# The gate projection of the latent branch moves from the end of one unit into the score tiles of its own

## The chip, the cores and the metric

The kernel runs on one NeuronCore of a Trainium2 chip. The metric is the device time of one execution in microseconds. Before the change it was 4350.89 us (median of three runs, 4349.49 to 4351.80).

## The reference

The input x (512 tokens of 1024 features) first passes a block with two attentions (dilated and two-dimensional neighbourhood) and a feed-forward part, and then two hybrid layers that also read a context of 256 tokens. Each layer projects the normalised tokens and runs three attention branches of width 1024; each branch is gated, projected, and merged. The change is almost all in the first branch, called mla (latent attention, 8 heads):

```
q  = (rms_norm(qc, q_norm) @ w_uq)    # per head 64 features plus 32 that are rotated
kv = (rms_norm(kvc, kv_norm) @ w_ukv) # per head 64 key features and 128 value features
s  = (q * 96**-0.5) . k               # keys: 512 latent tokens and 256 context tokens
o  = softmax(s) @ v                   # per head [tokens, 128]
y  = o * silu(z)                      # z = normalised tokens @ 128 columns of w_in per head
```

In the first layer the queries are all 768 tokens (six tiles of 128 queries, here called items), in the second only the 512 latent ones (four items). All is float32. A projection with the large matrices is done with three matmuls for each product (high times high, low times high, high times low), for which ScalarE (ACT) makes the high part of a weight tile and VectorE (DVE) the low part.

## The kernel before, in words

The program is a list of stages (`plan`, L119), each with its part on TensorE (PE), ACT, DVE and the DMA queue SP (SyncE). Every stage ends in a fence of the engines (L2292). The order of the work on each engine is the order in which the Python code issues it, and semaphores tie the engines together; nothing is scheduled by a planner, except that `done_by` (L727) says how many steps of a side task PE issues after each group of scores.

A stage "units" runs heads one after another: a prologue (projections of unit 0), a loop of steps (unit i, with the projections of unit i+1 beside it) and an epilogue (the last unit, nothing beside it). For mla there are eight units: a prologue, seven steps, an epilogue, in each of the two layers. The parts of a step on PE (`pe_units`, L1462 on), for unit i:

1. `pe_scores` (L731): for each item a score tile of 512 and 256 key columns, three matmuls each, into the PSUM banks 4 and 5 or 6 and 7 in turn. From the third group on, PE waits until ACT has taken the tile of two groups back (`exped`, L743). After each group it issues some side steps, and after the last group all that are left. The side steps are `qk_steps` of unit i+1 (L1018): the query projection (three K tiles, into banks 0 and 1) and the key projection (two K tiles, into banks 2 and 3). In front of the keys PE waits for `z_ev`, the gate of unit i having left banks 2 and 3 (L1026).
2. `pe_values` (L879): it waits until all probabilities are normalised, turns them chunk by chunk through PSUM (4 transposes, ACT or DVE copies them back in turn) and multiplies each with V. After the second turn it issues `pe_rope` (L1060), one matmul that rotates the queries of unit i+1 and waits for `rope_in`. Beside the products from the fourth on it issues one step of `v_steps` (the V projection of unit i+1, L1085) each. Steps that are left follow.
3. `pe_proj_z` (L1114): the gate projection of unit i+1 into banks 2 and 3: 8 K tiles, three matmuls each, of 512 columns and, in the first layer, again of 256.

ACT in a step (`act_units`, L1551): the exponentials of the items (L778); then `act_proj_qk` (L1132), which waits for the keys (`kv_ev`) and copies first the queries to SBUF (L1139) and then the keys' high part (L1141), after which `rope_in` is given; the copies of turned chunks 0, 2, 4, 6 (L993) with the queries' high part after chunk 4 (L1175); then `act_proj_z` (L1267): the high part of the next gate weight (L545) and the tanh of the gate (L1280), which waits for the gate's matmuls.

DVE in a step (`dve_units`, L1639): for each item the maximum (L803), and one item later the normalisation (L818, L821); the copies of chunks 1, 3, 5, 7 (L995), after chunk 1 the keys' low part (L1222) and the rotation (L1209 to L1212), after chunk 5 the queries' low part (L1196); the output (L1335); the copy of V (L1262); then `dve_proj_z` (L1283): the low part of the next gate weight (L555), and the gate's last step (L1293), which waits for the tanh.

In the stages dil and na of the first block, which have the same frame, the prologue's `act_proj_v` (L1236) makes the high part of weight 3, which is the first weight of unit 1, before it copies V's projection (L1244), and `dve_proj_v` (L1249) the low part before it copies the turned V (L1262). PE turns V in between (L1111) and then starts the scores.

## Time and profile before

| | |
|---|---|
| profiled execution, its own time | 4348.03 us |
| its span, first to last instruction | 4346.2 us |
| PE busy (matmul) | 3848.7 us, 89% |
| DVE busy | 2169.5 us, 50% |
| ACT busy | 1385.1 us, 32% |
| mean granted clock of TensorE | 0.948 |

How it is read: times are in microseconds from the start of the span. A row of the timeline has the start, the duration, the engine, the line, the operation, its output and inputs, how many alike follow each other, and in brackets how long the engine sat idle before it and what ended that. The granted clock is 1.00 at 2.4 GHz and 0.50 at 1.2 GHz. Matmuls are pipelined, so the distance of two starts tells more than a duration.

### The profile page before, as it was taken

What the parts mean: (1) busy time and instruction counts of PE and PEld (TensorE: products, weight loads), DVE (VectorE), ACT (ScalarE), POOL (GpSimd) and SP (SyncE); (2) the same over time, 40 slices, a digit from 0 to 9 for tenths busy, and PEclk for the clock granted to TensorE, in tenths of its full rate; (3) what the DMA queues carried; (4) which work ended last, traced back from release to release, by engine and by line L of the source; (5) the groups of instructions that cost most, each with busy time, mean ns of one, the idle gap of its engine ahead of it and who ended that gap; (6) DMA issues with size and microseconds to landing.
All of it is one profiled execution on the core that took longest, in us unless ns stands there. A gap on an engine that the chain in (4) does not pass through costs nothing. (4 is left out here: it accounts for less than half of the span.)

```text
span 4346.2 us, 56051 instructions
## 1 busy us (share of the span) xinstructions
PE 3848.7 (89%) x20877; PEld 2933.9 (68%) x20877; DVE 2169.5 (50%) x3457; ACT 1385.1 (32%) x2472; POOL 0.2 (0%) x4
## 2 busy tenths in 40 slices
PE   5988979997689999999798998976999999798898
PEld 2655758875466687777586766864667777576666
DVE  2555346543445525777524554243553677535544
ACT  2433233322223313444312433121332444314432
POOL 0000000000000000000000000000000000000000
PEclk8998989998799999999899999987999999899999
DMA  6443335531101021111121101211013121121122
GB/s 232 137 117 93 87 88 161 170 110 62 35 25 29 15 68 40 38 39 39 30 63 34 29 26 30 68 39 38 26 30 87 44 52 39 49 68 35 35 59 73
DMA packets 504242, 275.36 MB, mean 63 GB/s; under 512 B 56665, under 2 KB 489781, under 8 KB 504094
## 3 DMA queue, kind: packets, MB, share of 16 engines
q1 hardware_dynamic: 483186, 252.08, 20.7%
q10 hardware_dynamic: 20908, 21.26, 1.6%
q8 instruction: 99, 1.62, 0.2%
q14 instruction: 49, 0.40, 0.0%
HBM read 271.08 MB, written 10.32 MB: 65 GB/s over the span
## 5 line engine op out<-in xcount | busy, mean ns | idle before, releaser
L559 PE MATMUL ps<-h_high,w_high 128*128 128x512 f32 (+1 forms) x3512 | 1313.0, 374 | 165.8 <-DVEq L2294 129.8
L559 PE MATMUL ps<-h_low,w_high 128*128 128x512 f32 (+1 forms) x3512 | 1280.4, 365 | 0.0
L559 PE MATMUL ps<-h_high,w_low 128*128 128x512 f32 (+1 forms) x3512 | 1278.0, 364 | 0.0
L559 PEld LDWEIGHTS ps<-h_high,w_high 128*128 128x128 f32 x3512 | 673.4, 192 | 318.0 <-DVEq L2294 137.2
L555 DVE TENSOR_TENSOR w_low<-w_raw,w_high 128x1024 fp32r<-128x1024 f32 x378 | 453.6, 1200 | 629.9 <-ACT w_high L545 605.8
L559 PEld LDWEIGHTS ps<-h_high,w_low 128*128 128x128 f32 x3512 | 672.2, 191 | 106.6
L559 PEld LDWEIGHTS ps<-h_low,w_high 128*128 128x128 f32 x3512 | 673.8, 192 | 98.6 <-issue 2.2
L545 ACT ACTIVATE w_high<-w_raw 128x1024 fp32r<-128x1024 f32 x378 | 392.3, 1039 | 789.5 <-PE ps L559 606.2
L778 ACT ACTIVATE probs<-ps,neg_max 128x768 f32<-128x768 f32 (+2 forms) x368 | 289.1, 788 | 492.9 <-DVE neg_max L803 291.0
L559 PE MATMUL ps<-k_high,q_high 64*128 64x256 f32 (+4 forms) x784 | 189.9, 402 | 136.9 <-ACT probs L778 78.7
L559 PE MATMUL ps<-probsT,v 128*128 128x512 f32 (+4 forms) x736 | 287.5, 560 | 8.8 <-DVE probsT L995 8.6
L803 DVE TENSOR_REDUCE neg_max<-ps 128x1 f32<-128x768 f32 (+1 forms) x240 | 195.0, 846 | 113.5 <-PE ps L559 100.3
L559 PEld LDWEIGHTS ps<-k_high,q_high 64*128 64x128 f32 (+1 forms) x784 | 92.1, 193 | 228.8 <-ACT probs L778 118.1
L559 PE MATMUL ps<-y_high,w_high 128*128 128x512 f32 (+1 forms) x640 | 229.7, 359 | 1.3 <-ACT y_high L1971 1.1
L559 PE MATMUL ps<-y_low,w_high 128*128 128x512 f32 (+1 forms) x640 | 228.9, 358 | 0.0
L559 PE MATMUL ps<-y_high,w_low 128*128 128x512 f32 (+1 forms) x640 | 228.6, 357 | 0.0
L559 PE MATMUL ps<-y_and_merged 128*128 128x128 f32 (+4 forms) x656 | 168.0, 390 | 21.3 <-DVEq L2294 17.0
L799 DVE TENSOR_REDUCE row_max<-ps 128x1 f32<-128x512 f32 (+2 forms) x160 | 110.0, 688 | 149.3 <-PE ps L559 149.1
L887 PEld LDWEIGHTS ps<-ident,probs 128*128 128x128 f32 x832 | 103.2, 145 | 94.6 <-issue 77.5
L559 PE MATMUL ps<-k_low,q_high 64*128 64x256 f32 (+4 forms) x784 | 157.6, 333 | 0.0
L559 PE MATMUL ps<-k_high,q_low 64*128 64x256 f32 (+4 forms) x784 | 157.1, 332 | 0.0
L1978 ACT ACTIVATE probs<-ps 128x512 f32<-128x512 f32 x88 | 44.8, 538 | 336.3 <-PE ps L559 336.2
(200 smaller groups left out, 4034.7 us busy)
## 6 DMA issues: line engine op xcount, KB each, us to landing
w_raw<-in_w_in SPq DMA_DIRECT2D x444, 256.0 KB, 3.2
y_and_merged<-in_w_mod SPq DMA_DIRECT2D x96, 256.0 KB, 3.2
w_raw<-in_w_branch SPq DMA_DIRECT2D x96, 256.0 KB, 3.1
w_raw<-in_w_up SPq DMA_DIRECT2D x88, 256.0 KB, 4.2
y_and_merged<-in_w_ada SPq DMA_DIRECT2D x64, 256.0 KB, 3.3
w_raw<-in_w_out SPq DMA_DIRECT2D x48, 256.0 KB, 3.1
w_raw<-in_w_down SPq DMA_DIRECT2D x44, 256.0 KB, 3.0
y_and_merged<-in_w_ada SPq DMA_DIRECT2D x4, 2048.0 KB, 20.3
```

Source lines behind the costliest of these rows:

```text
L545: act.activation(WR[:, k, 0:nk], WRAW[:, k, 0:nk], ACT.Copy).then_inc(s_high, 1)
L555: nc.vector.tensor_tensor(WL[:, k, 0:nk], WRAW[:, k, 0:nk], WR[:, k, 0:nk].bitcast(F32), ALU.subtract).then_inc(s_low, 1)
L559: return nc.tensor.matmul(*a, **kw)
L778: act.activation(it["dst"], src, ACT.Exp, bias=NM[:, idx:idx + 1], accum_out=SL[:, idx:idx + 1]).then_inc(S["exped"], 1)
L799: v.tensor_reduce(MX[:, idx:idx + 1], src, AXX, ALU.max, negate=True)
L803: v.tensor_reduce(NM[:, idx:idx + 1], src, AXX, ALU.max, negate=True).then_inc(S["maxed"], 1)
L887: last = nc.tensor.transpose(PS[:, b:b + 128], tile, ident[:, :])
L1978: last = act.activation(d, p, ACT.Tanh, scale=0.5)
```

## The change

In mla the gate projection of a unit no longer stands at the end of the step before. Its steps (`mla_z`) are now the first side steps among the unit's own score groups, ahead of the query and key projection of the next unit; in the epilogue they are the only side steps, and in the prologue the gate is gone. PE waits for `kv_low` (new: the low part of the keys is made, so that banks 2 and 3 are free) before the first. ACT issues its part of the gate (`act_proj_z`) after the exponential of item `z_group`, DVE its part (`dve_proj_z`) after the maximum of that item and the normalisation of the item before; `z_group` comes out as item 3 of 0 to 5 in the first layer and as item 2 of 0 to 3 in the second. In the epilogue both do it after all items. `done_by` for mla has all but the last four side steps issued by the last group but one.

The query copy on ACT waits for `q_mm` (the query matmuls) instead of the keys, and gives `q_out` at once; the rotation matmul on PE waits for `q_out` instead of `rope_in`. The V projection of the next unit stands behind the values' last product on PE, not beside the products.

In the prologues of dil and na, ACT's high part and DVE's low part of weight 3 now follow the V copies.

```
@@ done_by
-            return max(n_side - TAIL, 0) * (group + 1) // (s["items"] // (2 if paired(s) else 1))
+            groups = s["items"] // (2 if paired(s) else 1)
+            if s["name"] == "mla":
+                return min(max(n_side - TAIL, 0) * (group + 1) // (groups - 1), max(n_side - TAIL, 0))
+            return max(n_side - TAIL, 0) * (group + 1) // groups
@@ dve_softmax, one item after another
                 if idx and s["name"] not in SCALED_LAST:
                     normalise(idx - 1)
+                after(idx)
@@ z_group
-            return min(g for g in range(s["items"] // 2) if done_by(s, nz + side_plan(s)[0], g) >= nz)
+            return min(g for g in range(s["items"] // (2 if paired(s) else 1)) if done_by(s, nz + side_plan(s)[0], g) >= nz)
@@ pe_rope
-            pe.wait_ge(S["rope_in"], cnt(s, "rope_in", t, ui, u + 1))
+            key = "q_out" if name == "mla" else "rope_in"
+            pe.wait_ge(S[key], cnt(s, key, t, ui, u + 1))
@@ act_proj_qk
+                act.wait_ge(S["q_mm"], cnt(s, "q_mm", t, ui, u + 1))
+                for d, p in evac_cols(s, 0, Q, cq, slice(0, 96)):
+                    last = act.activation(d, p, ACT.Copy, scale=sc)
+                last.then_inc(S["q_out"], 1)
                 act.wait_ge(S["kv_ev"], cnt(s, "kv_ev", t, ui, u + 1))
-                for d, p in evac_cols(s, 0, Q, cq, slice(0, 96)):
-                    act.activation(d, p, ACT.Copy, scale=sc)
@@ act_proj_v
-            if first:
+            if first and not s["first"]:
                 act_high(act, s, t, s["nh"], 3)
...
-            if s["first"] and not first:
+            if s["first"]:
                 act_high(act, s, t, s["nh"], 3)
@@ dve_proj_v
-                if s["first"] or first:
+                if s["first"] != first:
                     dve_low(dve, s, t, s["nh"], 3)
...
+            if s["first"] and first:
+                dve_low(dve, s, t, s["nh"], 3)
@@ pe_units
-                pe_proj_z(pe, s, 0, 0, 0)
+                if name == "diff":
+                    pe_proj_z(pe, s, 0, 0, 0)
...
+            def mla_z(t, u, i):
+                pe.wait_ge(S["kv_low"], cnt(s, "kv_low", t, 2, u + 1))
+                yield from split_steps(pe, s, t, 2, u, 128, tgroups(2, s["cq"]))
+            def mla_side(t, u, i):
+                yield from mla_z(t, u, i)
+                yield from qk_steps(pe, nxt, t, u, i + 1, True)
...
+                if name == "mla":
+                    pe_scores(pe, s, t, u, i, 0, mla_side(t, u, i), nz + n_side)
+                    pe_values(pe, s, t, u, i, 0, lambda: pe_rope(pe, nxt, t, u, name))
+                    for _ in v_steps(pe, nxt, t, u, i + 1):
+                        pass
+                    return
... (epilogue)
+                elif name == "mla":
+                    pe_scores(pe, s, t, u, i, 0, mla_z(t, u, i), nz)
@@ act_units and dve_units, in the step
+            def mla_z(t, u, i, idx):
+                if idx == z_group(s):
+                    act_proj_z(act, s, t, u, i)      # dve_proj_z on DVE
```

## Rows read from the trace of the kernel before

**Rows 1.** Windows: busy time of each engine, granted clock (PEclk), DMA share, GB/s.

```profile
1265.00:1301.00 36.00, 34.06 (x175) 24.14 (x174) 18.65 (x34) 11.22 (x25) 0.00 (x0) 1.00 0.09 25
...
700.00:800.00 100.00, 100.00 (x666) 81.43 (x665) 58.66 (x71) 34.90 (x48) 0.00 (x0) 1.00 0.57 164
```

**Rows 2.** Waits of PE, first layer's steps (two rows), second layer's (two rows).

```profile
PE ps L559 <- ACT probs L778: 9.7, 14, 0.9
PE ps L559 <- ACT k_high L1141: 4.7, 7, 0.7
...
PE ps L559 <- ACT probs L778: 4.7, 6, 1.0
PE ps L559 <- ACT k_high L1141: 2.4, 6, 0.4
```

**Rows 3.** Timeline of PE, first layer: a gate, then the next unit.

```profile
1292.28 0.48 PE L559 MATMUL ps<-h_high,w_high 128*128 128x512 f32 x1
...
1297.84 0.28 PE L559 MATMUL ps<-h_high,w_high 128*128 128x256 f32 x1
...
1300.71 0.40 PE L559 MATMUL ps<-k_high,q_high 96*128 96x512 f32 x1
...
1311.29 3.32 PE L559 MATMUL ps<-y_and_merged 128*96 128x256 f32 x10
...
1314.55 1.09 PE L887 MATMUL ps<-ident,probs 128*128 128x128 f32 x8
...
1316.32 1.10 PE L559 MATMUL ps<-qT,rot_mla 96*96 96x512 f32 x2 [0.68 <-ACT k_high L1141]
...
1327.24 1.05 PE L559 MATMUL ps<-y_and_merged 128*128 128x128 f32 x8
```

**Rows 4.** Timeline of ACT and DVE in the same unit.

```profile
1300.99 0.87 ACT L1280 ACTIVATE y_and_merged<-ps 128x512 f32<-128x512 f32 x2 [10.82 <-PE ps L559]
...
1301.89 1.02 DVE L1293 SCALAR_TENSOR_TENSOR y_and_merged<-y_and_merged,ps 128x512 f32<-128x512 f32 x2 [6.81 <-ACT y_and_merged L1280]
...
1303.49 1.82 DVE L803 TENSOR_REDUCE neg_max<-ps 128x1 f32<-128x768 f32 x2 [0.57 <-issue]
...
1309.79 0.90 ACT L778 ACTIVATE probs<-ps,neg_max 128x768 f32<-128x768 f32 x1 [0.92 <-DVE neg_max L803]
...
1312.88 0.35 DVE L821 TENSOR_SCALAR probs<-probs,exp_sum_inv 128x256 f32<-128x256 f32 x1
```

**Rows 5.** Page, costliest groups: busy, mean ns, idle before, releaser.

```profile
L555 DVE TENSOR_TENSOR w_low<-w_raw,w_high 128x1024 fp32r<-128x1024 f32 x378 | 453.6, 1200 | 629.9 <-ACT w_high L545 605.8
...
L545 ACT ACTIVATE w_high<-w_raw 128x1024 fp32r<-128x1024 f32 x378 | 392.3, 1039 | 789.5 <-PE ps L559 606.2
```

**Rows 6.** Timeline of PE, first layer: a score group after a wait.

```profile
1305.52 0.50 PE L559 MATMUL ps<-k_high,q_high 96*128 96x512 f32 x1 [0.82 <-ACT probs L778]
...
1305.86 0.40 PE L559 MATMUL ps<-k_low,q_high 96*128 96x512 f32 x1
```

**Rows 7.** Timeline of PE, first layer's epilogue: first score matmul, first turn.

```profile
1478.41 0.40 PE L559 MATMUL ps<-k_high,q_high 96*128 96x512 f32 x1
...
1490.71 1.97 PE L887 MATMUL ps<-ident,probs 128*128 128x128 f32 x8 [1.74 <-DVE probs L821]
```

**Rows 8.** Window inside that epilogue.

```profile
1486.00:1488.00 2.00, 1.05 (x4) 0.76 (x4) 1.92 (x5) 0.99 (x2) 0.00 (x0) 0.50 0.00 0
```

**Rows 9.** Timeline of PE, second layer's epilogue: first score matmul, first turn.

```profile
3238.67 0.40 PE L559 MATMUL ps<-k_high,q_high 96*128 96x512 f32 x1
...
3248.23 1.70 PE L887 MATMUL ps<-ident,probs 128*128 128x128 f32 x8 [3.55 <-DVE probs L821]
```

**Rows 10.** Timeline, prologue of dil (two rows) and of na (one row).

```profile
105.20 1.06 ACT L545 ACTIVATE w_high<-w_raw 128x1024 fp32r<-128x1024 f32 x1 [11.79 <-DMA w_raw<-in_w_in]
...
109.42 0.79 PE L559 MATMUL ps<-h_high,w_high 128*128 128x512 f32 x1
...
266.00 0.69 DVE L1262 COPY v<-ps 128x512 f32<-128x512 f32 x1 [6.06 <-PE ps L1111]
```

More of the change, by code:

```diff
@@ L151, in add @@
             now[k] = now.get(k, 0) + v
-    keys = ("h n square square_mm rstd scaled high x_t mm_ev rope_in rope_mm roped q_mm k_mm q_out kv_ev vt_in vt_mm v_ev z_ev tanh scores maxed exped normed "
+    keys = ("h n square square_mm rstd scaled high x_t mm_ev rope_in rope_mm roped q_mm k_mm q_out kv_ev kv_low vt_in vt_mm v_ev z_ev tanh scores maxed exped normed "
             "pt_act pt_dve rl_mm transposed o_done o_sq o_ss o_rs y bias merged up_ev gelu f_high f_low y_low y_high m_high m_low out_ev ctx_in mod_copy mod_sum qk_high qk_low").split()
@@ L176, in plan @@
             if s["name"] == "mla":
-                add(s, q_mm=n, k_mm=n, kv_ev=n, v_ev=n, z_ev=n, tanh=n, rope_mm=n, roped=n)
+                add(s, q_mm=n, q_out=n, kv_ev=n, kv_low=n, v_ev=n, z_ev=n, tanh=n, rope_mm=n, roped=n)
             if s["name"] == "diff":
@@ L1021, in qk_steps @@
                     for kc in range(3):
-                        mm(ps, WN[:, k, 96 * kc:96 * kc + 96], M[:, kc, lo:lo + n], start=kc == 0, stop=kc == 2)
+                        last = mm(ps, WN[:, k, 96 * kc:96 * kc + 96], M[:, kc, lo:lo + n], start=kc == 0, stop=kc == 2)
+                        if kc == 2 and (lo > 0 or not cq):
+                            last.then_inc(S["q_mm"], 1)
                         yield
@@ L1221, in dve_proj_qk @@
                     h = KH[0:64, 0:LAT] if d.shape[1] == LAT else KH[0:64, LAT:TOK]
-                    nc.vector.tensor_tensor(d, p, h.bitcast(F32), ALU.subtract)
+                    last = nc.vector.tensor_tensor(d, p, h.bitcast(F32), ALU.subtract)
+                last.then_inc(S["kv_low"], 1)
                 dve_rope(dve, s, u, t, ui, Q[0:96, 0:LAT], 96, 0, TAB["cos_mla"][:, :], TAB["sin_mla"][:, :])
@@ L1374, in moved @@
             m.base = dict(s.base)
-            for key, per in (("h", s["nh"]), ("n", s["nn"]), ("v_ev", 1), ("vt_in", 1), ("vt_mm", 1), ("z_ev", 1), ("q_out", 1), ("rope_in", 1), ("tanh", 1), ("kv_ev", 1),
+            for key, per in (("h", s["nh"]), ("n", s["nn"]), ("v_ev", 1), ("vt_in", 1), ("vt_mm", 1), ("z_ev", 1), ("q_out", 1), ("q_mm", 1), ("rope_in", 1), ("tanh", 1), ("kv_ev", 1), ("kv_low", 1),
                              ("qk_high", 1), ("qk_low", 1), ("roped", 2 if s["name"] == "diff" else 1), ("rope_mm", 2 if s["name"] == "diff" else 1), ("y", s["subs"])):
@@ L1540, in prologue @@
                 act_proj_v(act, s, 0, 0, 0, True)
-                if name != "swa":
+                if name not in ("mla", "swa"):
                     act_proj_z(act, s, 0, 0, 0)
@@ L1554, in mid @@
                         swa_z(t, u, i, idx)
+                    if name == "mla":
+                        mla_z(t, u, i, idx)
                     if name == "diff" and idx == side_plan(s)[1] - 1:
@@ L1584, in step @@
                         act_mod(act, s, i, s["nn"], e, 1, 384)
-                act_proj_z(act, nxt, t, u, i + 1)
+                if name != "mla":
+                    act_proj_z(act, nxt, t, u, i + 1)
             def epilogue(t, u, i):
                 act_exps(act, s, t, u, i, 0, splits(s, nxt, t, u, 0) if name == "swa" else [])
+                if name == "mla":
+                    act_proj_z(act, s, t, u, i)
                 if name == "swa":
@@ L1625, in dve_units, with mla_z @@
             nxt = moved(s)
+            def mla_z(t, u, i, idx):
+                if idx == z_group(s):
+                    dve_proj_z(dve, s, t, u, i)
             def swa_z(t, u, i, idx):
@@ L1635, in prologue @@
                 dve_proj_v(dve, s, 0, 0, 0, True)
-                if name != "swa":
+                if name not in ("mla", "swa"):
                     dve_proj_z(dve, s, 0, 0, 0)
@@ L1651, in step @@
                 dve_bias(dve, s, i)
-                dve_softmax(dve, s, t, u, i, 0, splits(s, nxt, t, u, 0), (lambda idx: swa_z(t, u, i, idx)) if name == "swa" else lambda idx: None)
+                dve_softmax(dve, s, t, u, i, 0, splits(s, nxt, t, u, 0), (lambda idx: (swa_z if name == "swa" else mla_z)(t, u, i, idx)) if name in ("mla", "swa") else lambda idx: None)
                 if name == "swa":
@@ L1665, in step @@
                     dve_proj_v(dve, nxt, t, u, i + 1)
-                dve_proj_z(dve, nxt, t, u, i + 1)
+                if name != "mla":
+                    dve_proj_z(dve, nxt, t, u, i + 1)
             def epilogue(t, u, i):
@@ L1670, in epilogue @@
                 dve_softmax(dve, s, t, u, i, 0, splits(s, nxt, t, u, 0) if name == "swa" else [])
+                if name == "mla":
+                    dve_proj_z(dve, s, t, u, i)
                 if name == "swa":
```

## The prediction

> **What bounds the kernel now.** I read the windows by stage first. In a step of the first mla stage PE is busy 34.06 of 36 us at a granted clock of 1.00, while DVE has 18.65 and ACT 11.22 [rows 1]: PE is the bound, and only its idle time can be won. The list of who waited for whom, taken over seven steps of each layer, says what that idle time is [rows 2]. In the first layer it is 9.7 us in 14 waits of score groups for an exponential (0.69 each, two a unit) and 4.7 us in 7 waits of the rotation matmul for ACT's key copy (0.67 each). In the second it is 4.7 us in 6 (0.78 each, one a unit) and 2.4 us in 6 (0.40 each). So a unit idles 2.06 us in the first layer and 1.18 us in the second; nothing else of note. The reader is to see that seven steps of each layer hold at most 14.4 and 8.3 us. The timeline then shows the edges: in the epilogues no side steps stand between the score groups, and PE idles with its clock down (their rows stand with the edges below).
>
> **The prices on PE.** A gate takes from 1292.28 to 1300.71, 8.43 us: 24 matmuls of 512 columns until 1297.84 (5.56 us, 0.23 each, 0.70 a step of three) and 24 of 256 (2.87 us, 0.12 each, 0.36 a step) [rows 3]. A score tile has the same columns (three of 512, three of 256): 1.05 us, or 0.36 for the 256-column tiles of the context's queries. The plain projections cost more: after the last group, one query step of 256 and four key steps (two of 512, two of 256) take from 1311.29 to 1314.55, 3.26 us for 1792 columns, so 0.93 for 512 and 0.47 for 256 [rows 3]. The keys are 2.8 us, the queries 4.2 in the first layer and 2.8 in the second.
>
> **The prices beside PE.** Maximum 0.91 (1.82 for two), exponential 0.90 and some 0.1 to its sum, tanh 0.87, last gate step 1.02, last normalisation of 256 columns 0.35 [rows 4]; high part 1.04, low part 1.20 [rows 5]. For the 512 columns of the second layer I take 0.60 for the tanh and 0.69 for the last step (estimates, two thirds).
>
> **A step of the first layer, laid out anew.** I write it from the first score matmul (0). Side steps by the new rule: 4, 4, 5, 4, 5 of 26 after the groups, then 4. Tile 0 to 1.05, four gate steps to 3.8; tile 1 and four to 7.7; tile 2 to 8.7 and five short ones to 10.5; tile 3 to 11.6, three gate steps (gate done at 12.7) and a query step to 13.6; tile 4 and five query steps to 17.2; tile 5 to 17.5; the keys to 20.3. Exponential 0 is over at 3.1, 2 at 10.7, 3 at 13.6: every group finds its bank free, so the two waits of 0.69 go. On ACT, after exponential 3: high part to 14.7, tanh to 15.5. On DVE: low part to 15.9, last step to 17.0. The keys may thus start at 17.0, and PE gets there at 17.5: no wait, 0.5 us to spare. Queued behind the gate's block on DVE are the maxima of items 4 and 5 and the last three normalisations: 17.4, 18.1, 18.5, 19.0, 19.8. PE asks for the probabilities at 20.3. Before, they were ready at 1313.2 against 1314.55 [rows 3, 4]; the slack shrinks from 1.3 to 0.5 us.
>
> The rotation: ACT is through with exponential 5 at 19.2, the query copy (0.86, as the tanh of the same columns) ends at 20.1, and PE's first two turns end at 21.2. The 0.67 us goes. The key copy moves behind it, 20.4 to 21.2, then chunk 0's copy to 21.8; PE's rotation ends at 22.1, so nothing new is late there, by 0.3 us.
>
> The V projection beside the products did no waiting of its own; its place at the end costs what it covered: chunk 7's short copy after a short product. I take 0.3 us for that and 0.1 for latencies elsewhere. At the end its 12 matmuls (four of them 1.05 us at most, 2.6 in all [rows 3]) cover the output on DVE (1.02), for which the next unit's scores wait; the copy of V ends as tile 0 does. PE also restarts slowly after a wait: its second matmul starts 0.34 after the first instead of 0.23 [rows 3, 6], so two restarts less are 0.2 more. So: 2.06 - 0.4 + 0.2, 1.9 us a step. Bounds: 0.9 (the two slacks of 0.5 missed by 0.5 each) and 2.3. Times seven: 13.3 us, from 6 to 16.
>
> **A step of the second layer.** Four tiles, 15 side steps: 3, 4, 4, 0, then 4. Tile 2 ends at 8.1, the last gate step at 8.8, three query steps at 11.6, tile 3 at 12.6. Exponential 2 ends at 10.2, high part 11.2, low part 12.5, last step 13.2: here the keys wait, 0.6 us. Maximum 3, exponential 3, its normalisation: 14.1, 15.1, 16.1, while the keys end at 16.0: another 0.1 to 0.2. So 0.8 us of new waiting against 1.18 and a restart of 0.1: 0.5 us a step, 3.4 us in all. Bounds: minus 0.5 a step (the block 1 us longer) and 1.2 (none of it felt): -3 to 8.
>
> This wait is DVE's order: the maximum of tile 3 stands behind the gate's last step. That is seen before too: tile 0 is complete 1.05 after 1300.71, but its maximum starts at 1303.49, behind the gate's step of 1301.89 [rows 3, 4].
>
> **The edges.** The prologues lose the gate: 8.4 and 5.6 us; the weight of unit 1 loses its early split and gains a later one, under scores. In the epilogues it fills waits. First layer before: 12.30 us from first score to first turn, with the clock at 0.50, so that eight transposes take 1.97 instead of 1.09 and the first product about 0.9 more [rows 3, 7, 8]: 14.1 in full-clock terms. After: side steps 2, 2, 3, 2, 3, then 4; PE is through at 13.5, the probabilities at 13.7. But ACT's gate part comes after all exponentials: high part until 14.1, tanh 15.0, chunk 0's copy 15.6, where PE wants it at 14.6; 0.2 more for chunk 1 behind DVE's low part and last step. That is 15.0, or +0.9: net -7.5 us. Second layer: 9.56 plus about 1.6 for the low clock [rows 9] against 10.0 plus 0.5: -0.7, net -6.3. Together 13.8 us; bounds 10 and 16.
>
> On the clock the trace shows 1.00 through steps that idle 0.7 to 1.0 us at a time [rows 1, 2], and 0.50 in the epilogue with its longer idling [rows 8]. With waits of about 1 us I count the new epilogues at full clock. The Trainium skill, in "TensorE: Matmul & The Clock Gate", section "What's actually happening", says that throttled is the default state and that recent activity releases it. By that rule a thin stretch can lose the clock without one long gap, which speaks against my count; the sum would then be some 3.5 us smaller.
>
> **Dil and na.** In dil's prologue ACT waited 11.79 us for weight 3's DMA, with V's copy queued behind. Now V, its turn and the first scores run during that wait. The next unit's projection then starts when weight 3 is split: 105.20 + 1.06 + 1.2 = 107.5 instead of 109.42 [rows 5, 10]: -1.9 us (0 to -3). In na the weight was there early; its low part of 1.2 us now stands on DVE behind V's copy, in front of the first maxima, and in front of PE's side steps [rows 5, 10]: +1.2 us (0 to 2.5). Together -0.7.
>
> **Sum.** 13.3 + 3.4 + 13.8 + 0.7 = 31.2 us. The profiled execution took 4348.03 (span 4346.2 and 1.8 around it), so 4316.8; the median of the runs shown lies 2.9 higher: 4320 us.
>
> **Rivals.**
> - *All waiting goes.* The gate's block is felt nowhere: 16 + 8 in the steps, 14 at the edges: 38 us, 4313. For it: 0.5 us of slack in the first layer. Against: the second layer's chain is longer than its cover by 0.6.
> - *Only the edges gain.* The waits in the steps are replaced by others as long (keys on `z_ev`, turns on the last normalisation): 14.5 us, 4336. For it: both slacks are near 0.5 us. Against: each link of the chain has a row.
> - *Slower: the gate's block becomes the path.* High part, low part, tanh and last step (1.04 + 1.20 + 0.87 + 1.02 = 4.1 us) run with nothing beside them in each unit, in front of the keys. The point is where the query steps that PE has left after the gate are shorter than the block and the softmax tail. A step would gain 2.06 and lose 4.1 in the first layer, 1.18 and 3.5 in the second: 14 + 16 = 30 us lost, 14.5 gained: 4366. Against: 4.6 us of scores and queries lie between the gate's end and the keys in the first layer, 3.8 in the second.
> - *A denser PE loses its clock.* Against: 100 us of 100 busy ran at 1.00 [rows 1]. At 0.50 for a tenth of the 14 steps (some 45 us at full speed) it would take 45 us more and make the kernel slower; I count it in the 0.03 of slower.
>
> **Chances.** Forecast (4310 to 4328) 0.68; all waiting goes 0.10; only the edges 0.17; slower 0.03; something between, no change, 0.02. A difference of 0.2%, 8.7 us, is about what can be told from no change. Faster 0.94, same 0.03, slower 0.03. The range 4309 to 4337 takes in the first two rivals.
>
> **What would show it.** In the first layer PE's waits for exponentials are nearly gone and a unit is 1.9 us shorter; the wait of the rotation is gone in both; the second layer shows a wait of the keys for L1293 of about 0.6 and a unit shorter by 0.5. The epilogue's clock stays at 1.00, with a wait of a product for L993 or L995 near 1 us. Dil's first scores come near 102. I am wrong if the waits reappear under L1293 or L821 with more than 1 us a unit.

## The result, and the profile after

The kernel after took 4307.39 us (median of four runs, 4305.82 to 4307.58) where the kernel before, on the same chip, took 4351.35 (4349.49 to 4357.63). The ratio is 0.9895, with a 95% interval from 0.988 to 0.991: 44 us faster. The forecast was 4320 with a range from 4309 to 4337, so the direction came out, most of the mechanisms did, and the size was 13 us too small. The profiled execution took 4305.82 us (span 4304.0); against the span of before that is 42.2 us, where the sum had 31.2.

The first view of the kernel after is the page's head: the span, then for each engine its busy time, share and instructions. The matmuls are as many as before. PE's busy time fell by 16.6 us, with the mean granted clock from 0.948 to 0.951; the other 25.6 of the 42.2 us were idle time. ACT is busy for 6.2 us more, 5.1 of them in four more loads of its function table (1.28 us each, two in each mla stage).

```profile
span 4304.0 us, 56060 instructions
...
PE 3832.1 (89%) x20877; PEld 2926.4 (68%) x20877; DVE 2169.0 (50%) x3457; ACT 1391.3 (32%) x2476; POOL 0.2 (0%) x4
```

To find the time I cut both traces at the fences of the stages and, inside the two mla stages, at the first score matmul of each of the eight units. The table gives us; "rest" is the span without the two mla stages. Such starts repeat: in a second profiled execution of the kernel after (e13 below) the two stages came out at 273.18 and 230.17.

| | before | after | change | forecast |
|---|---|---|---|---|
| layer 1: fence to first scores | 27.59 | 16.03 | -11.56 | -8.4 |
| layer 1: a unit, mean of seven | 35.49 | 33.02 | -2.47 | -1.9 |
| layer 1: last unit to the fence | 24.96 | 25.96 | +1.00 | +0.9 |
| layer 1: stage | 301.00 | 273.16 | -27.84 | -20.8 |
| layer 2: fence to first scores | 24.07 | 16.52 | -7.55 | -5.6 |
| layer 2: a unit | 28.11 | 27.68 | -0.43 | -0.5 |
| layer 2: last unit to the fence | 20.46 | 19.90 | -0.56 | -0.7 |
| layer 2: stage | 241.29 | 230.16 | -11.13 | -9.7 |
| rest | 3803.9 | 3800.7 | -3.2 | -0.7 |

The second view is the waits of PE over the seven steps of each layer, in total us, times, longest. In the first layer the list is empty: the 14 waits for exponentials and the 7 for the key copy [rows 2] are gone. In the second layer those are gone too, and two others stand there, the ones forecast: 0.54 a unit for the gate's last step and 0.24 for the last normalisation.

```profile
PE ps L559 <- DVE y_and_merged L1306: 3.8, 7, 0.5
PE ps L891 <- DVE probs L824: 1.7, 7, 0.3
```

The third view is the timeline of one unit of the second layer, all engines, in order of start. The gate's last step on DVE ends at 3015.56 and the keys start at 3015.61; behind that step stand on DVE the maximum of the last item, its normalisation, and behind that the turns. The rotation (3019.59) has no wait.

```profile
3012.66 1.04 ACT L545 ACTIVATE w_high<-w_raw 128x1024 fp32r<-128x1024 f32 x1
...
3013.61 0.59 ACT L1293 ACTIVATE y_and_merged<-ps 128x512 f32<-128x512 f32 x1
3013.74 1.23 DVE L555 TENSOR_TENSOR w_low<-w_raw,w_high 128x1024 fp32r<-128x1024 f32 x1 [1.24 <-ACT w_high L545]
...
3014.88 0.68 DVE L1306 SCALAR_TENSOR_TENSOR y_and_merged<-y_and_merged,ps 128x512 f32<-128x512 f32 x1
...
3015.61 2.79 PE L559 MATMUL ps<-y_and_merged 128*64 128x512 f32 x8 [0.54 <-DVE y_and_merged L1306]
3015.73 0.96 DVE L806 TENSOR_REDUCE neg_max<-ps 128x1 f32<-128x768 f32 x1 [0.17 <-issue]
...
3018.66 1.09 PE L891 MATMUL ps<-ident,probs 128*128 128x128 f32 x8 [0.25 <-DVE probs L824]
...
3019.59 1.02 PE L559 MATMUL ps<-qT,rot_mla 96*96 96x512 f32 x2
```

The epilogues keep their clock. These windows (columns as in [rows 1]) of the first layer's epilogue have 1.00 where the window of before had 0.50 [rows 8], and the turns at 1462.36 take 1.09 for eight instead of 1.97 [rows 7]. The products behind them wait for the copies of ACT and DVE, with 0.47 and 0.16 us listed. By the starts it is 0.7 and 0.4: the first product stands 1.57 us behind the first turn, where eight turns at 0.11 would make 0.88, and the second turned pair 1.72 behind the first, where one further on has 1.30. The forecast had charged 1.0 and 0.2 for the two.

```profile
1458.00:1460.00 2.00, 2.00 (x18) 1.91 (x17) 1.91 (x5) 1.09 (x3) 0.00 (x0) 1.00 0.03 8
...
1462.00:1464.00 2.00, 1.22 (x10) 0.93 (x9) 1.65 (x3) 1.88 (x4) 0.00 (x0) 1.00 0.00 0
```

```profile
1462.36 1.09 PE L891 MATMUL ps<-ident,probs 128*128 128x128 f32 x8 [0.31 <-DVE probs L824]
1463.93 1.12 PE L559 MATMUL ps<-probsT,v 128*128 128x512 f32 x2 [0.47 <-ACT probsT L997]
1465.65 1.13 PE L559 MATMUL ps<-probsT,v 128*128 128x512 f32 x2 [0.16 <-DVE probsT L999]
```

The last view is the prologue of the first layer. The rotation starts straight behind the keys, and V's 24 records take 2.94 us at a clock of 1.00.

```profile
1207.04 3.53 PE L559 MATMUL ps<-y_and_merged 128*96 128x256 f32 x11
1210.50 1.10 PE L559 MATMUL ps<-qT,rot_mla 96*96 96x512 f32 x2
1214.60 2.94 PE L559 MATMUL ps<-y_and_merged 128*128 128x128 f32 x24 [3.00 <-DVE qT L1222]
```

The questions were four: what made the first layer's prologue 3.2 us better than the gate's 8.4; what made a unit of the first layer 0.6 better than forecast; what the two small parts (V, dil and na) are worth; and whether the waits left in the second layer can go.

### The profile page after: what moved, and what is told of

Same layout as the page of the kernel before. It is cut to its first block and busy times, and to the rows that moved or that the text cites. A ratio compares the mean times of both kernels' runs of the same rounds, so it can differ in the third digit from the quotient of the medians.

```text
span 4304.0 us, 56060 instructions
## 1 busy us (share of the span) xinstructions
PE 3832.1 (89%) x20877; PEld 2926.4 (68%) x20877; DVE 2169.0 (50%) x3457; ACT 1391.3 (32%) x2476; POOL 0.2 (0%) x4
## 5 line engine op out<-in xcount | busy, mean ns | idle before, releaser
L559 PE MATMUL ps<-y_and_merged 128*128 128x128 f32 (+4 forms) x656 | 152.4, 384 | 26.8 <-DVEq L2341 17.0
```

Of the source, the lines that this page charges most:

```text
L559: return nc.tensor.matmul(*a, **kw)
```

## The experiments

The first four ran on one chip and share the runs of the kernel before (median 4350.33), so do the next four (4355.59) and the last three (4352.64). This table has what the texts below refer to, in us, cut as above; "ratio" is to the kernel before on the same chip, and L1 and L2 are here the first and the second layer.

| | time | ratio, 95% interval | L1 fence to scores | L1 unit | L1 stage | L2 fence to scores | L2 unit | L2 stage | rest |
|---|---|---|---|---|---|---|---|---|---|
| e1 dil and na only | 4351.37 | 1.0000 (0.9991 to 1.0009) | | | 300.97 | | | 241.38 | 3808.0 |
| e2 after, queries late | 4325.75 | 0.9945 (0.9931 to 0.9959) | 19.18 | 33.98 | 282.97 | 18.08 | 28.07 | 234.45 | 3806.6 |
| e3 after, V beside | 4312.87 | 0.9917 (0.9904 to 0.9931) | 16.01 | 33.32 | 275.22 | 16.51 | 27.49 | 228.83 | 3804.7 |
| e4 after, tanh first | 4312.06 | 0.9919 (0.9906 to 0.9933) | 16.07 | 33.02 | 273.54 | 16.51 | 27.58 | 230.20 | 3806.1 |
| e5 gate only | 4325.19 | 0.9929 (0.9916 to 0.9943) | 19.18 | 34.27 | 285.02 | 18.06 | 27.87 | 233.00 | 3807.5 |
| e6 queries only | 4342.33 | 0.9968 (0.9957 to 0.9979) | 24.49 | 34.60 | 293.07 | 22.10 | 27.57 | 236.85 | 3803.6 |
| e7 prologues wait | 4312.82 | 0.9902 (0.9887 to 0.9917) | 19.22 | 33.03 | 276.39 | 18.06 | 27.75 | 232.16 | 3805.1 |
| e10 gate early | 4302.98 | 0.9882 (0.9867 to 0.9897) | 16.01 | 33.02 | 273.11 | 16.54 | 27.05 | 225.73 | 3803.3 |
| e11 and V beside in L2 | 4306.11 | 0.9890 (0.9874 to 0.9906) | 16.03 | 33.02 | 273.17 | 16.53 | 26.85 | 224.34 | 3805.5 |
| e12 and epilogues | 4319.21 | 0.9919 (0.9905 to 0.9933) | 16.02 | 33.03 | 279.12 | 16.55 | 26.85 | 231.07 | 3808.4 |
| e13 after again | 4308.85 | 0.9901 (0.9885 to 0.9917) | 16.06 | 33.02 | 273.18 | 16.50 | 27.69 | 230.17 | 3799.9 |

### e2: the queries' part taken out

```
-            key = "q_out" if name == "mla" else "rope_in"
+            key = "rope_in"
...
                 act.wait_ge(S["q_mm"], ...)
+                act.wait_ge(S["kv_ev"], ...)
                 for d, p in evac_cols(...):
                     last = act.activation(d, p, ACT.Copy, scale=sc)
                 last.then_inc(S["q_out"], 1)
-
-                act.wait_ge(S["kv_ev"], ...)
```

> The kernel after, but the queries are again copied after the keys, and the rotation waits for the key copy. Theory (a wait costs its listed idle time and some 0.2 us of drain that the list leaves out, and in the first prologue it also keeps the clock down): a unit of the first layer 33.02 -> 33.9 us, one of the second 27.68 -> 28.3, the prologues +3.5 and +1.7 us: 7 x 0.89 + 7 x 0.6 + 5.2 = 15.6 us more than after, 4323. Rival (the prediction as it stood: only the listed idle of the steps, 4.7 + 2.4, nothing in the prologues): 7 us more, 4314.5, prologues within 0.3 of after's 16.03 and 16.52.

The two stages are 14.1 us longer than after (9.8 and 4.3), the time 18 us (its rest is longer too). The theory holds and the rival falls: the prologues lose 3.15 and 1.56 us, the units 0.96 and 0.39. The waits of PE show 5.2 us in seven, 0.74 each, for those 0.96, so 0.22 us of each wait is not in the list.

```profile
PE ps L559 <- ACT k_high L1150: 5.2, 7, 0.7
```

In the second layer the list has almost nothing (0.2 us in one wait) for the 0.39 a unit. Its timeline says why. The idle of a PE row is counted from the modelled end of the matmul before, here 3037.17 + 1.10, and the rotation starts at 3038.41, with no bracket of its own; only the weight load shows the wait. Yet from the turns to the first product it is 2.18 us (3037.17 to 3039.35), and 1.79 in the kernel after, by its own rows 3018.66 and 3020.45. The distance of two starts has the loss, the idle column doesn't.

```profile
3037.17 1.10 PE L891 MATMUL ps<-ident,probs 128*128 128x128 f32 x8 [0.25 <-DVE probs L824]
...
3038.41 0.24 PEld L559 LDWEIGHTS ps<-qT,rot_mla 96*96 96x96 f32 x2 [0.38 <-ACT k_high L1150]
3038.41 1.10 PE L559 MATMUL ps<-qT,rot_mla 96*96 96x512 f32 x2
...
3039.35 1.02 PE L559 MATMUL ps<-probsT,v 128*128 128x512 f32 x2
```

### e7: only the prologues wait for the key copy

```
+        def pe_rope(pe, s, t, u, name, first=False):
...
-            key = "q_out" if name == "mla" else "rope_in"
+            key = "q_out" if name == "mla" and not first else "rope_in"
...
+                if first:
+                    act.wait_ge(S["kv_ev"], ...)
```

> The kernel after, but in the prologues alone the queries are copied after the keys and the rotation waits for the key copy, as before. Theory (this wait brings TensorE's granted clock down in front of V's 24 matmuls, so it costs more than its own length): first layer's prologue 16.0 -> 19.0 us with a window at 0.50 behind the rotation, second layer's 16.5 -> 18.2; units as after; 4312. Rival (the wait costs its length only and the clock stays at 1.00): 16.0 -> 17.9, 16.5 -> 18.2, 4311 with V's records at 2.9 us. The window of the clock tells them apart, not the sum.

The prologues come out 3.19 and 1.54 us longer, and the units as after. In the first layer the wait is back with 1.78 us, and V's 24 records take 4.91 us.

```profile
1213.30 3.54 PE L559 MATMUL ps<-y_and_merged 128*96 128x256 f32 x11
1218.62 1.30 PE L559 MATMUL ps<-qT,rot_mla 96*96 96x512 f32 x2 [1.78 <-ACT k_high L1153]
1222.06 4.91 PE L559 MATMUL ps<-y_and_merged 128*128 128x128 f32 x24 [2.15 <-DVE qT L1224]
```

The windows of e7 show the clock at 1.2 GHz under those records; PE had been busy 1.30 of 2 us and then not at all. In the kernel after it idles 3.00 us in front of V, more than the 2.15 here, and the clock stays at 2.4 GHz. What differs is the idle of 1.78 us ahead of the rotation, with which it is 3.93 us of idle in two pieces instead of 3.00 in one.

```profile
1218.00:1220.00 2.00, 1.30 (x2) 0.24 (x2) 1.06 (x3) 0.56 (x2) 0.00 (x0) 0.85 0.00 0
1220.00:1222.00 2.00, 0.00 (x0) 0.00 (x0) 1.93 (x3) 0.00 (x0) 0.00 (x0) 0.50 0.00 0
1222.00:1224.00 2.00, 1.94 (x9) 1.95 (x10) 0.96 (x2) 1.95 (x2) 0.00 (x0) 0.50 0.00 0
```

```profile
1213.00:1215.00 2.00, 0.40 (x3) 0.40 (x4) 1.47 (x3) 0.42 (x1) 0.00 (x0) 1.00 0.00 0
...
1215.00:1217.00 2.00, 2.00 (x20) 2.00 (x20) 0.96 (x1) 1.70 (x2) 0.00 (x0) 1.00 0.00 0
```

(The second pair is the kernel after.) So the 3.2 us are one wait in the prologue, part of it as lost clock: V's records are 1.97 us longer. They don't simply add to the wait, for the 0.85 us less of waiting in front of V gives some back. All five kernels with the wait have this low clock in the first layer's prologue, and none of the eight profiles without it.

In the second layer it is not so clean. There the clock is at 0.50 under V's first records even in the kernel after, with the same 3.00 us of idle in one piece and none ahead of the rotation; the wait of 1.51 us in e7 makes V's records 5.49 us long instead of 4.57. Why 3.00 us cost the clock in one prologue and not in the other, no run here settles.

```profile
2998.21 4.57 PE L559 MATMUL ps<-y_and_merged 128*128 128x128 f32 x24 [3.00 <-DVE qT L1222]
```

### e6 and e5: the parts alone

e6 is the kernel before with the two edits of the queries (the early copy, the wait on `q_out`).

> The kernel before, with only the queries' part: copied to SBUF as soon as their matmuls are done, the rotation waits for that. Theory (a wait is worth its listed idle and some 0.2 us of drain): the waits of the rotation go in both layers, 0.67 and 0.40 listed, with the drain 0.87 x 7 + 0.6 x 7, and 1.76 + 0.2 and 1.49 + 0.2 in the two prologues: 13.9 us, of which 8 in the first mla stage and 5.9 in the second; 4337. Rival (the listed idle alone): 7.1 + 3.3 = 10.4 us, 4340.5. Second rival (the early copy on ACT delays exponentials or the key copy, so that other waits grow): less than 7 us.

The ratio gives 13.9 us, but the stages only 7.9 and 4.4, 12.4 together where the theory had 8 and 5.9; that the ratio hits the number is chance. The units (-0.89 and -0.54) are as the theory had them. The first prologue is not: it is 3.10 us shorter where the theory had 1.96, since its wait also cost the clock (e7), and the second 1.97 for 1.69. The epilogues are 1.4 and 1.3 us longer than before, though nothing in them is changed; in the first layer's the clock stays low for 5.6 us behind the first turn instead of 3.4. They more than take back what the prologues gained beyond the theory. That the waits for exponentials are still 9.7 us in 14 shows that the early copy does not disturb the exponentials.

e5 is the kernel after less the queries' part, V's move, and dil and na.

```
-                    pe_values(pe, s, t, u, i, 0, lambda: pe_rope(pe, nxt, t, u, name))
-                    for _ in v_steps(pe, nxt, t, u, i + 1):
+                    values = v_steps(pe, nxt, t, u, i + 1)
+                    pe_values(pe, s, t, u, i, 0, lambda: pe_rope(...), values, 3)
+                    for _ in values:
... (and e2's edit; dil and na as before)
```

> The kernel after without three of its parts: the queries are copied after the keys and the rotation waits for the key copy, V of the next unit stands beside the products, dil and na are as before. Only the gate's move is left. Theory (parts add up; queries' part 14 us in the two mla stages, as their removal alone showed, V's part 1 us, dil and na 2 us at most): the mla stages 18 and 8 us shorter than before instead of 27.8 and 11.1, less 2 for V in the first layer, so 24 us faster than before, 4326. Rival (parts cover each other: with the gate gone from the prologue the key copy is what PE waits for, and V beside the products hides part of that wait): the mla stages together at least 5 us off the 24, 4321 or 4331.

The stages are 15.98 and 8.29 us shorter than before, 24.3 together. The theory's sum holds: in the first layer 15.98 for the gate, 9.81 for the queries (e2) and 2.06 for V (e3) make 27.85 of 27.84 measured. In the second 8.29 + 4.29 - 1.33 make 11.25 of 11.13. The gate alone takes 8.41 and 6.01 us from the prologues, against the 8.4 and 5.6 of the forecast, and 1.22 from a unit of the first layer. In that 1.22 a new wait is charged: with V beside the products and no gate behind them, the next unit's scores wait for the output on DVE, 2.9 us in seven.

### e3: V beside the products again

The edit is the first hunk of e5's diff, on the kernel after.

> The kernel after, with the V projection of the next unit beside the values' products again, as before. Theory (from the unit times: the 0.3 us a step that the prediction charged for V at the end did not show): no difference, 4306 to 4308.5, units 33.0 and 27.7 us. Rival A (the charge was real, and something else gained more): 14 x 0.3 = 4 us faster, 4303. Rival B (V at the end is itself a gain, because its evacuation or its 12 matmuls cover the output of DVE before the next scores): a wait of the next unit's scores for DVE's output of up to 0.7 us a unit, 4312 or more.

Neither text fits alone. In the first layer a unit is 0.30 us longer: with V beside the products, the next unit's scores wait for the output on DVE.

```profile
1255.37 0.47 PE L559 MATMUL ps<-k_high,q_high 96*128 96x512 f32 x1 [0.43 <-DVE y_and_merged L1348]
```

In the second a unit is 0.19 shorter, with no such wait: there V at the end is a loss. 2.06 lost and 1.33 won leave 0.7 us; that the time is 5 us above after's is mostly its rest, 3804.7 for 3800.7. The forecast had charged V's move 0.3 a step in the first layer and nothing in the second; e3's text took the charge for both. Rival B is what the first layer shows; its number, 4312 or more, was hit by the rest.

### e1: dil and na alone

The edit is the change's own hunks of `act_proj_v` and `dve_proj_v`, on the kernel before.

> The kernel before, with only the prologues of dil and na changed. Theory (the terms on record): dil 1.9 us shorter, since its first side steps start at 107.5 instead of 109.42, na 1.2 us longer, together -0.7 us, so 4350.6 where the kernel before takes 4351.3. Rival: in the full change dil's stage became 0.5 and na's 1.7 us shorter; if this part did that, the time falls by 2.2 us, and na's first side steps start no later than before.

No difference: 1.0000, from 0.9991 to 1.0009. Dil's stage is 0.4 us shorter (164.54 for 164.93), na's 0.2. Of the waits of PE in dil's stage, the first two here are of the kernel before, the last two of e1.

```profile
PE ps L1111 <- ACT probs L1244: 6.3, 1, 6.3
PE ps L559 <- DVE neg_max L796: 6.1, 3, 2.2
```

```profile
PE ps L559 <- DVE w_low L555: 5.1, 1, 5.1
...
PE ps L1111 <- ACT probs L1244: 0.7, 1, 0.7
```

The wait of 6.3 us became two, 5.1 and 0.7. Dil's first side step starts 1.7 us earlier from the fence (28.6 against 30.3 us), the scores of the later units 1.2 us earlier up to the last unit's (132.3 against 133.6). There the clock takes most of it: it falls to 0.50 at 134.6 us from the fence instead of 138.4, and 0.5 us is left where the last unit's products start.

Na's +1.2 is there too, though its stage hides it. The first side step now stands 2.08 us behind the first scores instead of 0.90, behind a wait for the low part of weight 3 as the prediction has it, and the second and third units start 1.1 and 1.2 us later from the fence than before. The first row is of the kernel before, the others of e1.

```profile
266.79 0.50 PE L559 MATMUL ps<-h_high,w_high 128*128 128x512 f32 x1
```

```profile
263.38 0.50 PE L559 MATMUL ps<-k_high,q_high 64*128 64x512 f32 x2
...
265.46 0.47 PE L559 MATMUL ps<-h_high,w_high 128*128 128x512 f32 x1 [1.11 <-DVE w_low L555]
```

(Before, the first scores start at 265.89.) The last unit starts 0.4 us earlier than before, because in the third unit the kernel before has its clock at 0.50 for a while, 100 us behind the fence, and e1 has not. The two windows are of before and of e1, at the same distance from the fence. All three kernels with na's old prologue (before, e5, e6) have this dip and none of the others.

```profile
344.00:346.00 2.00, 2.00 (x7) 1.51 (x6) 1.69 (x10) 1.63 (x4) 0.00 (x0) 0.50 0.00 0
```

```profile
341.50:343.50 2.00, 2.00 (x11) 1.37 (x9) 1.92 (x6) 0.82 (x3) 0.00 (x0) 1.00 0.00 0
```

So the theory had both mechanisms right, na's with its size and dil's with 1.2 of the 1.9 us. That the two stages together are 0.6 us shorter, for its 0.7, is luck, since the clock moved both. The rival, that na's side steps start no later, falls.

### e4 and e10: the waits left in the second layer

e4 puts, in mla, ACT's tanh ahead of the next weight's high part and DVE's last step ahead of the low part.

```
@@ act_proj_z (the same in dve_proj_z with dve_low)
-            if s["name"] != "swa":
+            if s["name"] == "diff":
                 act_high(act, s, t, per, off + 1)
... (tanh)
+            if s["name"] == "mla":
+                act_high(act, s, t, per, off + 1)
```

> The kernel after, in mla ACT makes the tanh of the gate ahead of the next weight's high part, and DVE the gate's last step ahead of the low part. Theory: the gate leaves banks 2 and 3 about 2.2 us sooner, so the second layer's wait of the keys for the gate's last step (0.55 us listed) and of the turns for the normalisation (0.26) go, with the drain 0.8 to 1.0 us a unit, and each epilogue's chain gets some 1 us shorter: 7 x 0.9 + 2 = 8 us faster than after, 4299. In the first layer a unit stays at 33.0 us, since PE waits nowhere there. Rival: the next weight's split, now behind the gate, is late for the query steps of the side work; PE then waits for w_low instead, as long or longer: 4307 to 4318.

Missed: the time lies in the rival's range, but PE does not wait for the low part of a weight, and of the 4.7 us above the kernel after the rest alone has 5.4. The waits of the keys are gone, but those of the turns have grown from 1.7 to 5.2 us, and a unit is 27.58 instead of 27.68. The epilogues are 0.35 and 0.7 us longer.

```profile
PE ps L891 <- DVE probs L824: 5.2, 7, 0.8
```

The order inside the gate's block doesn't change what stands on DVE ahead of the last maximum. e10 moves the block instead:

```
@@ done_by, for mla
+                up = 0 if s["cq"] else groups - 2
-                return min(max(n_side - TAIL, 0) * (group + 1) // (groups - 1), max(n_side - TAIL, 0))
+                return min((max(n_side - TAIL, 0) * (group + 1) + up) // (groups - 1), max(n_side - TAIL, 0))
```

> The kernel after, with the side steps of mla's second layer rounded up: 4, 4, 3, 0 after the groups instead of 3, 4, 4, 0, so that the gate's steps are done with the second group and ACT and DVE make the gate after item 1 instead of item 2. Theory (the gate's block, high part to last step, stands in front of the last maxima on DVE, and is the cause of both waits left in the second layer): its last step ends near 9.3 us from the first score matmul instead of 13.2, the keys wait no more and the last normalisation is done at 14.9, before the keys end at 15.4. The waits of 0.55 and 0.26 us go, a unit falls from 27.68 to 26.6 us, 7 us in seven, 4300. Rival (DVE's sum of work in front of the turns is the bound, wherever the gate stands, as it was when the tanh went first and the wait went over from the keys to the turns): the wait of the turns grows to 0.7 and the unit stays at 27.6, 4307.

The unit falls to 27.05, by 0.63 us of the 1.08 expected; the stage is 4.4 us shorter than after's. The wait for the gate is gone, that for the last normalisation stays as it was, and the rival falls.

```profile
PE ps L892 <- DVE probs L825: 1.7, 7, 0.2
```

It took 4302.98 us at a ratio of 0.9882 (0.9867 to 0.9897); e7 on the same chip took 4312.82. It has the best time of all kernels here, but its interval overlaps that of the kernel after (0.988 to 0.991, and 0.9885 to 0.9917 in e13).

### e11, e12 and e13

e11 adds V beside the products in the second layer alone.

> The kernel after with the side steps of the second layer rounded up (4, 4, 3, 0, gate made after item 1), and in the second layer alone V of the next unit beside the products. Theory (the two act on different waits): V beside the products saved 0.19 us a unit in the second layer when it was alone and cost 0.30 in the first, where it is left at the end; so the second layer's unit goes from 27.05 to 26.86 us, its stage to 224.4, 1.3 us less. Rival (with the keys on time, the next unit's first scores come earlier and now wait for DVE's output, as in the first layer): unit 27.05 to 27.2.

The unit is 26.85 and the stage 224.34, 1.4 us less than e10, as expected; the time, 4306.11, doesn't show it, since its rest is 2.2 us longer (3805.5 against 3803.3).

e12 moves the gate's block in the epilogues ahead of the last item.

```
-                    pe_scores(pe, s, t, u, i, 0, mla_z(t, u, i), nz)
+                    pe_scores(pe, s, t, u, i, 0, mla_z(t, u, i), nz + TAIL)
@@ the epilogues of ACT and DVE: act_proj_z and dve_proj_z from behind all items to
+                last_z = lambda idx: ... if name == "mla" and idx == s["items"] - 2 else None
```

> As the one before, and in both epilogues of mla all gate steps stand among the score groups and ACT and DVE make the gate after the last item but one, ahead of the last exponential and the last maximum, where they did it after all items. Theory (the epilogue's turns wait for copies queued behind the gate's work): first layer's epilogue 25.96 -> 24.9 us, second's 19.9 -> 19.0, 2 us together. Rival (the last maximum now waits for the gate's last step, and the chain maximum, exponential, normalisation is what the turns wait for): no change or up to 1 us longer each.

Far off: the epilogues are 6.0 and 6.7 us longer (31.92 and 26.56). The rival's mechanism is right and its size isn't. The timeline of the first layer's epilogue shows it. PE is through with its scores at 1469.7. The high part, the low part (1.22) and the last step (1.01) stand ahead of a maximum of 0.42 us for which everything waits, and two normalisations behind that; PE idles 4.40 us, the clock falls and eight turns take 1.97.

```profile
1469.44 0.28 PE L559 MATMUL ps<-k_high,q_low 96*128 96x256 f32 x1
1470.04 0.86 ACT L1294 ACTIVATE y_and_merged<-ps 128x512 f32<-128x512 f32 x2
1470.17 1.22 DVE L555 TENSOR_TENSOR w_low<-w_raw,w_high 128x1024 fp32r<-128x1024 f32 x1 [0.76 <-ACT w_high L545]
1471.32 1.01 DVE L1307 SCALAR_TENSOR_TENSOR y_and_merged<-y_and_merged,ps 128x512 f32<-128x512 f32 x2
...
1472.42 0.42 DVE L807 TENSOR_REDUCE neg_max<-ps 128x1 f32<-128x256 f32 x1
...
1474.12 1.97 PE L892 MATMUL ps<-ident,probs 128*128 128x128 f32 x8 [4.40 <-DVE probs L825]
```

This is the slower rival of the prediction in small: the gate's block on the path with nothing beside it.

e13 is the kernel after, run again.

> The kernel after once more, for two questions. First, how far its stages repeat: theory: the two mla stages at 273.2 and 230.2 within 0.3 us, its units at 33.02 and 27.68. Second, whether the 3.2 us that it gained outside the two mla stages are its own: theory: they are not, stages that the change does not touch come in two lengths 1.5 us apart by the execution, and the rest of the span comes out 3803 to 3808 us instead of 3800.7. Rival: the rest repeats at 3800.7 within 1 us.

The two mla stages repeat within 0.03 us. The rest comes to 3799.9 against 3800.7, inside the rival's 1 us. But that agreement is a sum of differences both ways: four stages of the same code differ by 1.0 to 1.7 us between the two executions (the first block's output stage 46.2 and 47.9, the last part of its feed-forward 127.8 and 126.6, and two behind it). And the whole time of a kernel moves more than that. The four executions of e13 took 4305.1 to 4313.8 us, the eleven of e1 4341.49 to 4354.99; both profiles of the kernel after are of its fastest execution of the four. So whether the 3.2 us outside mla are this kernel's own stays open. What is known of them: 2.3 lie in dil and na, which are 0.5 and 1.7 us shorter in both executions, and na's is the clock's (one low stretch gone and another shorter), against the work's +1.2. The seven other variants of the kernel after that have the change's code in all those stages have 3803.3 to 3808.4. Single stages at the same code mostly differ by 1.3 to 1.7 us between profiles, the output stage by up to 2.8. One is the stage behind the second layer's mla: 93.33 us in the kernel after, 91.72 in e11. These are its windows from 3230, first of the kernel after and then of e11; PE is busy throughout in both, and the clock differs.

```profile
3230.00:3232.00 2.00, 2.00 (x7) 1.53 (x6) 1.83 (x3) 0.00 (x0) 0.00 (x0) 0.59 0.56 133
3232.00:3234.00 2.00, 2.00 (x7) 1.59 (x6) 0.01 (x1) 0.00 (x0) 0.00 (x0) 0.56 0.68 201
```

```profile
3230.00:3232.00 2.00, 2.00 (x11) 1.64 (x10) 1.31 (x2) 0.00 (x0) 0.00 (x0) 1.00 0.87 224
3232.00:3234.00 2.00, 2.00 (x11) 1.65 (x10) 0.00 (x0) 0.00 (x0) 0.00 (x0) 1.00 0.70 210
```

What decides whether the clock falls there isn't settled.

## Why the prediction was too small

Two steps failed: the prologues' term left a wait out, and the steps' term took listed idle time for lost time. The other mechanisms were right. The mis-sized terms went nearly all in one direction, and two came out beyond their own bounds (steps of the first layer 17.3 us, bound 16; the edges 18.7, bound 16). The gap of 11.0 us between the two profiled executions splits into 7.0 in the first layer, 1.4 in the second and 2.5 elsewhere.

- **The prologues: 5.1 of the 11.0 us.** "The prologues lose the gate: 8.4 and 5.6 us" is the first step that failed, by what it left out: it put the queries' wait there at nothing, without a reason. The gate is worth 8.41 and 6.01 (e5). But the queries' edit acts in the prologue as well, where nothing covers the key copy. There it is worth 3.15 and 1.56 us (e2; 3.19 and 1.54 in e7), as much in the first layer as three steps. I had read the waits over the seven steps only. The row of this wait stands in the trace of before: it is 1.76 us, and V's records behind it run at 1.2 GHz.

```profile
1213.44 1.30 PE L559 MATMUL ps<-qT,rot_mla 96*96 96x512 f32 x2 [1.76 <-ACT k_high L1141]
```

- **The steps of the first layer: 4.0 us.** "So a unit idles 2.06 us" and "seven steps hold at most 14.4" took the list of waits for the whole loss: the second step that failed. Cut at starts (means of seven units, before and after), it is 21.99 and 20.04 us from the first score to the first turn, the gate counted in: 1.95 us for two waits listed with 1.38. From the first turn to the first product it is 2.71 and 1.79: 0.92 for one wait listed with 0.67; e2 has 0.96 for 0.74. So removing 2.06 listed was worth 2.87, and 0.2 of the 0.8 more was in the sum, as slow restarts. The trace of before shows it for one wait: from the side step at 1301.76 to the second score matmul it is 1.10 us where nothing waits, and 2.18 from 1303.68 to 1305.86 [rows 6] with 0.82 listed.

```profile
1301.76 1.02 PE L559 MATMUL ps<-y_and_merged 128*96 128x512 f32 x2
...
1302.86 0.40 PE L559 MATMUL ps<-k_low,q_high 96*128 96x512 f32 x1
...
1303.68 1.02 PE L559 MATMUL ps<-y_and_merged 128*96 128x512 f32 x2
```

  The 0.4 charged against it was right: from the first product to the next gate or scores it is 10.80 us before and 11.19 after, 0.39 more. That V at the end saves 0.30 in e3 is no contradiction. Before, the gate stood between the values and the next scores and covered the output on DVE; e3 has neither gate nor V there.
- **The steps of the second layer: the sum right, two of its terms by luck.** Forecast -0.5 a unit, measured -0.43; waits of 0.6 and 0.1 to 0.2 forecast, 0.54 and 0.24 found. The chain high part, tanh, low part, last step, maximum came out link by link, with ends within 0.2 us of the rows of the timeline above, and from the first score to the first turn, the gate counted in, it is 16.17 us before and 16.12 after, for -0.1 forecast. But the rotation's wait was worth 0.65 (2.44 to 1.79) for 0.40 listed, and V at the end costs 0.27 (9.50 to 9.77), which the forecast had at nothing here; the two errors cancel.
- **The epilogues: right**, +1.0 and -0.56 for +0.9 and -0.7. The first turn comes 13.9 us behind the first score for 13.7 forecast, and 10.2 for 10.0. The doubt about the clock did not come true: the trace has 1.00 through both. The Trainium skill's page "TensorE: Matmul & The Clock Gate", section "What's actually happening", has recent activity as what releases the throttle; the epilogues after agree with it, as does e12, where 4.40 us without a matmul brought 0.50.
- **Dil and na: the work near the forecast, the stages not.** Forecast -1.9 and +1.2; at the scores of the later units e1 has -1.2 and +1.2, at the stages' ends -0.4 and -0.2, and the change -0.5 and -1.7. The low stretches of the clock make the difference. That the sum of -0.7 was near e1's -0.6 is luck.
- **Outside mla: 2.5 us**, of which 1.6 are in dil and na. The rest of the span differs by up to 8 us between kernels and is not explained beyond the clock's dips. The median of the forecast, too, was set 2.9 us over the profiled execution; the measured one lies 1.6 over.

The rivals: "all waiting goes" is true of the first layer and false of the second; "only the edges gain" and the slower ones are refuted by the table. Even the 38 us of "all waiting goes" fall short of the 42.2 measured, since it was made from the same list. The queries' part alone was worth 14.1 us, which the forecast had at some 7. For the range this means that a bound made from the list of waits was no bound: the terms that rest on it missed together, and the range was too narrow below.

## What to carry to other kernels

Price a wait by the distance of two starts around it, against the same two where there is no wait; the idle column left out some 0.25 us of each here, and nearly all of a 0.39 us loss in the second layer. When an edit removes a wait in a loop, read the same wait in the prologue and the epilogue too, where nothing covers it and where the clock can go with it. When a block of work moves in an engine's queue, its place counts against the softmax links queued behind it: one item earlier won 4.4 us in seven steps, another order within the block nothing, and in an epilogue with nothing beside it, the block ahead of the last item instead of behind it lost 6. A term that seems to have missed by the time of its stage may be there at the starts, with the clock against it, as na's was.

## What the runs showed of the hardware

- Idle time of the same length had two prices. With 3.00 us in one piece in front of V, the granted clock stayed at 1.00 in the first layer's prologue of the kernel after and was 0.50 under V's first records in the second's. With 1.78 us before the rotation and 2.15 behind it, V ran at 0.50 in the first layer too.
- Stages at the same code mostly differ by 1.3 to 1.7 us between profiles, by one dip of the granted clock more or less. Some dips go with the kernel (na's stage is 161.81 and 161.78 us in two executions of the kernel after, 163.3 to 163.7 in the eleven other profiles), others differ between two executions of it. The rest of the span moved by 8 us over twelve kernels, and the time of one kernel by up to 13.5 over its executions. Edits worth less than that are told apart by the starts in their own stage, not by the time.
